# Turning the scaled rows between two layers by SBUF transfers and VectorE's 32x32 transposes, in a two-layer float32 kernel on one core

## What is computed

```python
for i in range(2):
    h = rms_norm(x, pre_norm[i])              # rows scaled by 1/sqrt(mean square), columns by pre_norm
    proj = h @ w_in[i]                        # token mixer, memory query and gate columns
    kv = rms_norm(mem, mem_norm[i]) @ w_kv_mem[i]
    ...                                       # short convolution (layer 0) or differential attention (layer 1),
    ...                                       # cross-attention into kv, gates
    y = branch @ w_out[i]
    x = x + rms_norm(y, post_norm[i])
```

## Time and profile before

| | |
|---|---|
| median of 3 runs | 961.62 us |
| the profiled execution | 961.81 us |
| its span on the core | 959.8 us |
| TensorE matmul busy | 942.2 us, 98% |
| VectorE busy | 629.6 us, 66% |
| ScalarE busy | 476.5 us, 50% |
| transfers | 182.3 MB, mean 190 GB/s; queue of the loads 59.6% of 16 engines |

### The profile page before, as it was taken

One profiled execution on the slowest core, in us unless ns is written; L12 is line 12 of the kernel. 1 busy time (PEld: TensorE's weight loads), 2 busy tenths in 40 slices (PEclk: granted clock), 3 DMA queues, 4 the chain that ended last, 5 costly groups with the idle time before them and its releaser, 6 DMA issues.

```text
span 959.8 us, 14019 instructions
## 1 busy us (share of the span) xinstructions
PE 942.2 (98%) x5129; PEld 809.8 (84%) x5129; DVE 629.6 (66%) x872; ACT 476.5 (50%) x720; POOL 1.2 (0%) x9
## 2 busy tenths in 40 slices
PE   6999999999999999999999999999999999999996
PEld 5888888888888888888888888888888888888885
DVE  4777656666665666655596447457878878886555
ACT  6866544444434444344465445435465465554441
POOL 0000000000000000000000000000000000000000
PEclk9999999999999999999999999999999999999999
DMA  9666465566666565666566656565655765746562
GB/s 313 218 220 216 143 209 175 175 199 189 203 193 187 188 195 185 207 196 195 183 217 194 192 154 195 159 204 168 197 178 156 221 180 164 206 147 204 191 194 90
DMA packets 149690, 182.30 MB, mean 190 GB/s; under 512 B 8017, under 2 KB 118929, under 8 KB 148881
## 3 DMA queue, kind: packets, MB, share of 16 engines
q1 hardware_dynamic: 148704, 177.25, 59.6%
q10 hardware_dynamic: 944, 4.49, 1.3%
HBM read 176.48 MB, written 2.10 MB: 186 GB/s over the span
## 4 chain that ended last, share of the span: by engine, by line
PE 96%; DVE 1%; ACT 1%; issue 1%; DMA 1%; DVEq 0%; ACTq 0%
PE psum L345 42%; PE psum L346 21%; PE psum L374 9%; PE psum L373 9%; PE psum L372 9%; PE psum L391 1%; PE psum L542 1%; PE psum L416 1%; PE psum L399 1%; DMA cross_gate<-in_mem_norm_dram 1%; PE psum L514 0%; PE psum L408 0%; DVE memT_split L849 0%; PE psum L525 0%; PE psum L524 0%
## 5 line engine op out<-in xcount | busy, mean ns | idle before, releaser
L345 PE MATMUL psum<-hT_split,hi_ring 128*128 128x512 f32 x1600 | 560.0, 396 | 0.0
L821 DVE TENSOR_TENSOR lo_ring<-raw_ring,hi_ring 128x1024 fp32r<-128x1024 f32 x320 | 387.2, 1223 | 251.5 <-ACT hi_ring L591 248.4
L591 ACT ACTIVATE hi_ring<-raw_ring 128x1024 fp32r<-128x1024 f32 x320 | 337.6, 1062 | 401.0 <-PE psum L346 266.2
L346 PE MATMUL psum<-hT_split,lo_ring 128*128 128x256 f32 x1600 | 444.6, 278 | 0.0
L345 PEld LDWEIGHTS psum<-hT_split,hi_ring 128*128 128x128 f32 x1600 | 300.1, 188 | 70.8 <-issue 2.0
L346 PEld LDWEIGHTS psum<-hT_split,lo_ring 128*128 128x128 f32 x1600 | 300.9, 188 | 0.1
L372 PE MATMUL psum<-hi_ring,branchT_split 128*128 128x512 f32 x256 | 99.9, 390 | 0.0
L374 PE MATMUL psum<-hi_ring,branchT_split 128*128 128x512 f32 x256 | 99.6, 389 | 0.0
L373 PE MATMUL psum<-lo_ring,branchT_split 128*128 128x512 f32 x256 | 99.6, 389 | 0.0
L373 PEld LDWEIGHTS psum<-lo_ring,branchT_split 128*128 128x128 f32 x256 | 48.1, 188 | 10.0
L374 PEld LDWEIGHTS psum<-hi_ring,branchT_split 128*128 128x128 f32 x256 | 48.0, 188 | 10.0
(11 more groups left out here) (169 smaller groups left out, 623.7 us busy)
## 6 DMA issues: line engine op xcount, KB each, us to landing
raw_ring<-in_w_in_dram SPq DMA_DIRECT2D x224, 512.0 KB, 4.2
raw_ring<-in_w_out_dram SPq DMA_DIRECT2D x64, 512.0 KB, 4.9
raw_ring<-in_w_kv_mem_dram SPq DMA_DIRECT2D x32, 512.0 KB, 5.5
layer_area<-layer_area SPq DMA_DIRECT2D x48, 64.0 KB, 3.2
stage_area<-in_mem_dram SPq DMA_DIRECT2D x4, 512.0 KB, 7.7
x_residual<-in_x_dram SPq DMA_DIRECT2D x1, 2048.0 KB, 10.7
x_residual<-in_x_dram ACTq DMA_DIRECT2D x1, 2048.0 KB, 8.4
layer_area<-in_post_norm_dram ACTq DMA_DIRECT2D x2, 1024.0 KB, 5.4
```

Of the source, the lines that this page charges most:

```text
L345: mm(o, hi[:, k, P * c:P * (c + 1)], X[:, kt, :], start=kt == 0, stop=False)
L346: last = mm(o[:, SEQ:], lo[:, k, P * c:P * (c + 1)], X[:, kt, 0:SEQ], start=False, stop=kt == KT - 1)
L591: run(whi[:, slot, :], raw[:, slot, :], ACT.Copy).then_inc(hi_ready, 1)
L821: V_.tensor_tensor(wlo[:, slot, :], raw[:, slot, :], whi[:, slot, :].bitcast(f32), SUB)\
```

## The change

Turning is moved off TensorE. The scaled rows are copied inside SBUF by 32 transfers (two row tiles x 16 pairs of a 32-row band and a 32-column band), so that each 32-row band of the result holds the blocks of its 32 columns; VectorE then transposes within 32x32 blocks (8 instructions of 128x512) into `h1T`, and the two engines make the high and low halves from there instead of from PSUM. Both areas lie in XC. 16 of the transfers are issued by SyncE, 8 ahead of the load of unit 4 and 8 ahead of that of unit 5 of G_VM1; 16 by ScalarE, in front of items 0 and 1 of G_VM1. VectorE's transposes stand in front of items 2 and 3, the halves in front of items 4 and 6, on both engines. The squares of the first row tile move in front of the last high half of G_KM1, and `scale_x` to the front of G_KM1 + 1.

```diff
+    quads = nc.alloc_sbuf_tensor_at("h1_quads", [P, KT, SEQ // 32, 32], f32, offset=xc_at).ap()
+    h1T = nc.alloc_sbuf_tensor_at("h1_turned", [P, KT, SEQ], f32, offset=xc_at + 4 * KT * SEQ).ap()
...
+    def to_quads(q, t, blocks):
+
+        for tb, b in blocks:
+            to = quads[32 * b:32 * b + 32, :, 4 * t + tb, :]
+            rows = y_all[32 * tb:32 * tb + 32, t, :].rearrange("r (k b c) -> r k b c", k=KT, b=4)[:, :, b, :]
+            q.dma_start(to, rows).then_inc(quads_loaded[t], 16)
+
+    QUAD_BLOCKS = [(tb, b) for tb in range(4) for b in range(4)]
...
+        def first_quads(i):
+            sp.wait_ge(xs_ready, TT + 1)
+            to_quads(sp, 0, QUAD_BLOCKS[i:i + 8])
...
-            row_group(u + 2 * B_UNITS, w_kv_mem[l], CROSS_WIDTH, in_order)
+            row_group(u + 2 * B_UNITS, w_kv_mem[l], CROSS_WIDTH, in_order,
+                      at={4: lambda: first_quads(0), 5: lambda: first_quads(8)} if l else {})
...
-        row_group(G_VM1, U_VM1, G_VM1 % 2, XB, in_order,
-                  at={1: turns_of(N_H1, range(4), y_all, lambda: pe.wait_ge(xs_ready, 4)),
-                      4: turns_of(N_H1, range(4, 8), y_all)})
+        row_group(G_VM1, U_VM1, G_VM1 % 2, XB, in_order)
...
+        def turned_h1(n):
+
+            act.wait_ge(h1_turned, 4 + n // 2 + 1)
+            for kt in (2 * n, 2 * n + 1):
+                last = run(XA[:, kt, 0:256], h1T[:, kt, :], ACT.Copy, scale=gT[:, KT + kt:KT + kt + 1])
+            last.then_inc(tr_hi, 1)
...
-        column_group(G_KM1, U_KM1, G_KM1 % 2)
-        for t in range(TT):
+        def new_squares(t):
             act.wait_ge(x_new, t + 1)
             squares(xres[:, t, :], y_all[:, t, :], ss[:, 2 + t:3 + t], x_squared)
+
+        column_group(G_KM1, U_KM1, G_KM1 % 2, at={3: lambda: new_squares(0)})
+        new_squares(1)
...
+        def last_quads(i):
+            act.wait_ge(xs_ready, 2 * TT)
+            to_quads(act, 1, QUAD_BLOCKS[i:i + 8])
+
         row_group(G_VM1, U_VM1, G_VM1 % 2, vm, scale=mem_rstd,
-                  at={1: steps_of(N_H1, range(4), XA, KT), 4: steps_of(N_H1, range(4, 8), XA, KT)})
+                  at={0: lambda: last_quads(0), 1: lambda: last_quads(8),
+                      4: lambda: [turned_h1(n) for n in range(4)], 6: lambda: [turned_h1(n) for n in range(4, 8)]})
...
-                     at={2: lambda: scale_x(4, y_all)})
+                     at={0: lambda: scale_x(4, y_all)})
...
+        def turn_quads(t):
+
+            dve.wait_ge(quads_loaded[t], 16 * len(QUAD_BLOCKS))
+            for c in range(4):
+                V_.transpose(h1T[:, 4 * c:4 * c + 4, P * t:P * (t + 1)], quads[:, 4 * c:4 * c + 4, 4 * t:4 * t + 4, :])\
+                  .then_inc(h1_turned, 1)
...
+            dve.wait_ge(tr_hi, N_H1 + n + 1)
+            for kt in (2 * n, 2 * n + 1):
+                last = V_.scalar_tensor_tensor(XA[:, kt, 256:512], h1T[:, kt, :], gT[:, KT + kt:KT + kt + 1],
+                                               XA[:, kt, 0:256].bitcast(f32), MULT, SUB)
+            last.then_inc(tr_lo, 1)
+
+        row_group(U_VM1, at={2: lambda: turn_quads(0), 3: lambda: turn_quads(1),
+                             4: lambda: [turned_h1(n) for n in range(4)], 6: lambda: [turned_h1(n) for n in range(4, 8)]})
```

More of the change, by code:

```diff
@@ L195, in build @@
     xs_ready = sem("xs_ready")
+    quads_loaded, h1_turned = [sem(f"h1_quads_loaded{t}") for t in range(TT)], sem("h1_turned")
     angle_ready, table_ready = sem("angle_ready"), sem("table_ready")
@@ L229, in column_group, with row_group @@
                      w[:, B_KT * n:B_KT * (n + 1), bass.ds(col, BCOLS)])
-        def row_group(u, w, col, order):
+        def row_group(u, w, col, order, at={}):
             w = w.rearrange("(k p) n -> p k n", p=P)
             for n, k in enumerate(order):
+                if n in at:
+                    at[n]()
                 unit(u + n, n % SLOTS, raw[:, n % SLOTS, :].rearrange("p (k c) -> p k c", k=A_KT),
@@ L1046, in _, with turned_h1 @@
         column_group(G_KM1 + 1, columns_before(G_KM1, 5) + 1, U_KM1 + B_UNITS, (G_KM1 + 1) % 2, kmT[:, 2:4, :],
-                     at={2: lambda: scale_x(4, y_all)})
+                     at={0: lambda: scale_x(4, y_all)})
         scale_keys(1)
-        row_group(U_VM1, at={1: steps_of(N_H1, range(4), XA, KT), 4: steps_of(N_H1, range(4, 8), XA, KT)})
+        def turn_quads(t):
[3 more added lines that the diff above has]
+                  .then_inc(h1_turned, 1)
+        def turned_h1(n):
+            dve.wait_ge(tr_hi, N_H1 + n + 1)
[5 more added lines that the diff above has]
+                             4: lambda: [turned_h1(n) for n in range(4)], 6: lambda: [turned_h1(n) for n in range(4, 8)]})
         for i in range(2):
```

## The result

The changed kernel takes 966.56 us (median of 5 runs, 965.22 to 966.91) against 961.62 for the kernel before; the ratio is 1.0049, with a 95% interval of 1.0034 to 1.0064. So it is slower by 4.9 us. The profiled execution took 966.67 us, with a span of 964.9 (before: 961.81 and 959.8).

What follows compares the result with a forecast made beforehand. TensorE, busy 98% of the span, was taken as the bound. Removing transposes saves 3.5 us, a stall adds 4.3: 0.8 slower, so 962.6 from the profiled 961.81, 962.4 as median; range 958.0 to 968.0.

Steps and rivals of the forecast that it cites:

- scaling sooner, V0 just in time: Squares and scaling moved forward in VectorE's order; first weight unit of G_VM1 ready at 495.0 for 495.14, cost 0 to 0.1.
- V5: Weight unit 5 of row group G_VM1 (units 0 to 7); TensorE was to want it at 508.8.
- T: Time when ScalarE's high half of V5 is done: 498.6 + 16p, predicted 508.7.
- Q0: First weight unit of G_QM1, the group after G_VM1; TensorE was to want it at 516.95 (before: 520.4).
- stall up to Q0: TensorE's wait because VectorE's chain reaches Q0 at T + 12.6: 16p - 5.75, so 4.3 us.
- Rival D: VectorE's eight transposes take two passes, 1.23 instead of 0.60 each, 5.0 us more: 967.4; chance 0.06.
- p: Queue time of one added transfer, issue to next issue, on SP or ScalarE: 0.37 to 0.63, taken as 0.63.
- Rival B: Short issues: a transfer holds its queue like a weight load, p = 0.42, stall 1.0, time 959.1; chance 0.30.
- the point where the engines decide: Cost c per piece where 494.15 + 0.77c + 2.8 + 1.06 passes 508.7: 14 ns; 10 ns was assumed.
- Rival C: Small pieces bind the transfer engines: 22 ns a piece, stall 10.5, time 968.6; at 17 ns, 964.8; chance 0.22.
- The 494.15: Starting time in the sum for V5's data: 494.15 + 16.9 + 2.8 = 513.9 at 22 ns a piece.
- the case I held likeliest for its size (within 0.2%): Time within 1.9 us of no change: chance 0.39, of which 0.37 from the forecast's own case.

## Why the prediction was right or wrong

The time lies in the range, at its upper side, and 4.2 us above the forecast. The sum's terms, one by one:

| step | predicted | measured |
|---|---|---|
| transposes removed | 3.5 | gone; without the transfers 4.1 faster (interval 2.7 to 5.2) |
| scaling sooner, V0 just in time | 0 to 0.1 | nothing |
| first batch on SP | 5.0 | 5.5 |
| issue of V4's load | 0.4 | 0.7 |
| second batch on SP | 5.0 | 7.4 |
| landing of V5 | 4.4 | 5.4 |
| first issue to end of V5's high half (T) | 15.9 | 20.05 |
| a 128x512 transpose on VectorE, step | 0.60 | 0.60 |
| from T to Q0 | 12.6 | 13.0 |
| stall up to Q0 | 4.3 | 8.8 |
| landing of the second tile's transfers | not in the sum | holds VectorE for 0.23 |

- The mechanism was right in the main: what stalls TensorE is the late high half of V5 and then VectorE's chain to Q0, which ran as written, with 2.48 us for four transposes and 13.0 us in all. Rival D (two passes a transpose) is out. One path was left out: the sum never asks when the second tile's transfers land. They landed at 517.03, 0.23 us after VectorE wanted them, and so the chain that ended last runs through them and not through V5. That the forecast's path came to nearly the same length is luck.
- The step that was mis-sized is "T = 492.75 + 16p + 0.4 + 4.4 + 1.06 = 498.6 + 16p" with p = 0.63 on both batches and 4.4 for the landing: 2.4 of the 4.1 us came in the second batch, 1.0 in the landing, 0.5 in the first batch and 0.3 in the issue of V4's load. Rival B's short issue (0.42) never occurred. The issue in the changed kernel is 0.59 at the least, and 0.60 in the median with a quarter of the pieces, so the earlier trace rows gave the right base. The trace's answer on line L223, SP's issues (ns min/median/max, first and last start), of the changed kernel and then of the one with a quarter of the pieces:

```profile
L223 SPq DMA_DIRECT2D h_quads<-stage_area x16: 592/634/2512, 492.0 to 505.0; - x16
```

```profile
L223 SPq DMA_DIRECT2D h_quads<-stage_area x16: 592/602/870, 492.7 to 503.8; - x16
```

  The push-back shows in the longest issue: 2.5 us against 0.87.
- What I left out is that the two limits add to each other when they are close. I took 10 ns a piece from the row of the 12-byte pieces of conv_w and put the point where the engines decide at 14 ns. The 10 ns were right for engines that carry only such pieces (9.6 in the kernel with half the transfers). In the changed kernel's three windows, where loads pass too, 64 us of engine time each, less the loads' bytes at 26 GB/s an engine, come to 13 to 15 ns for each of some 4,000 small pieces. That is an estimate and an upper bound, since it takes the engines to be never idle; it lies where my comparison of two totals put the turning point, and by that comparison there was still hardly any push-back. Of 4.1 us by which T was late, 3.2 vanish with three quarters of the pieces. A reading that fits is that the engines' work comes in lumps, while both queues issue, and the loads wait behind the lump; no run shows it by itself, and the run with GpSimd's queue doesn't fit it. Rival C, "at 17 ns, 964.8", was closer to what happened than the forecast, and two of its signs came (low GB/s at full share, VectorE waiting for the transfers), but its price of a piece did not. The 494.15 from which its formula starts is given without a row.
- The stall was placed too late in the text: 4.5 us of it fall before V5 and only 1.5 before Q0, since T came out 4 us later than assumed. The formula for Q0 still holds within 0.4 us, because VectorE's chain behind T has a gap of 0.23 us only: T = 512.07 and 13.0 more are Q0's 525.11.
- The Trainium skill (DMA: Bandwidth & Descriptors, "Why small descriptors are slow (HBM only)") was on the cheap side, an estimate of 6.2 us for all 2 MB from its 78% of a link, which it states for a remote transfer. The trace disagrees for these moves within SBUF: at 9.6 ns, 16,384 pieces take 9.8 us of 16 engines, and the same bytes in pieces of 512 bytes let V5 be ready 2.4 us sooner. The same page's table of specifications in the Trainium skill, by which pieces under 512 bytes fall below line rate, agrees with that.
- The chances: the case I held likeliest for its size (within 0.2%) didn't come; the side slower by more than 0.2% did, which had 0.31.

## What to carry to other kernels

Work taken off a full engine pays only if the ones that take it over can carry it while they also feed that engine. Before turning or regrouping data by transfers inside SBUF, count three things apart: the issues, each of which holds its queue (and every load or activation written behind it); the pieces, which share the engines with the loads; and the landing of the last transfer, which the consumer waits for. Where one is near its limit, move the half whose result is wanted last, and leave the other half where it was.

## What the runs showed of the hardware

- A transfer from SBUF to SBUF over 32 partitions holds SP's or ScalarE's queue for 0.59 us at the least. The medians are 0.60 (SP) and 0.62 (ScalarE) with 128 pieces, 0.63 and 0.70 with 512; a weight load takes 0.37. GpSimd's queue took 0.65 each.
- With nothing else on the 16 engines a piece of 128 bytes takes one of them 9.6 ns, 215 GB/s in all (half the transfers, 500 to 504). A share of 1 doesn't mean that they are at this limit: the changed kernel's windows had it with 152 to 209 GB/s.
- TensorE's granted clock fell to half, from 2.4 to 1.2 GHz, after the 4.3 us gap before V5. Windows of the changed kernel (PEclk is the third number from the end):

```profile
513.00:514.00 1.00, 0.62 (x3) 0.54 (x4) 1.00 (x3) 0.67 (x1) 0.00 (x0) 0.97 1.13 343
514.00:515.00 1.00, 1.00 (x4) 0.80 (x3) 1.00 (x2) 0.69 (x1) 0.00 (x0) 0.50 1.16 315
```

  The matmuls of V5 then step by 0.43 us instead of 0.23 (513.95 to 517.35 for eight), some 1.6 us lost on TensorE. Here that is covered: VectorE's low half of V7 ends at 519.47 + 1.18 = 520.65, and TensorE, half clock or not, starts V7 right behind it, at 520.71.
